# Four weight pairs of a head by seven block products in place of two, in a hybrid recurrent and attention layer

## The chip, the cores and the metric

The kernel runs on one core of a Trainium2 chip. The metric is the time of one execution on the device, in microseconds, as the median of three runs. The core's engines are TensorE (PE in the profile; its weight loads are PEld), VectorE (DVE), ScalarE (ACT), GpSimd (POOL) and SyncE (SP). They work side by side and wait for each other by semaphores. SP and POOL issue DMAs.

## What is computed

One decoder layer over 512 tokens and 16 meta tokens in front of them, with 1024 channels and 8 heads of 128 in each of two branches. Cut to what matters:

```
u = rmsnorm(h, norm_g)
proj = einsum('bld,de->ble', u, w_in)                 # 1024 -> 10 x 1024
hq, hf, hi, hz, aq, ak, av, az, ga, gb = split(proj)
oA = hgrn2_chunked(hq, log f(hf), 1 - f, hi)           # per head, recurrent
yA = (rmsnorm(oA) * silu(hz)) @ w_branch_a
oB = diff_attention(rope(aq), rope(ak), av, lam)       # per head, two softmaxes
yB = (rmsnorm(oB) * silu(az)) @ w_branch_b
m = sigmoid(ga) * yA + sigmoid(gb) * yB
out = rmsnorm(h + m @ w_out, final_g)                  # the 512 tokens
```

The large part is `proj`. Every projection works on full fp32 values that are split in two: a high part (`w_hi`, `uT_hi`, rounded to the type that TensorE multiplies in one pass) and the rest (`w_lo`, `uT_lo`). One product of a 128x128 weight tile is three matmuls: high by high, low by high and high by low (`three`).

## The kernel before, in words

A head needs eight blocks of 128 weight columns: HF, HQ (the recurrent forget gate and query), AK, AQ (attention key and query), HI, HZ (recurrent value and output gate), AV, AZ (attention value and output gate). The kernel makes them in two ways.

A **unit** is one block of 128 columns against all eight tiles of the contraction, over all 528 or 512 tokens: 48 matmuls of 256 to 272 columns or 24 of 512. In every head HI, HZ, AV and AZ are units (`unit`, `section`), in this order.

A **pair** is two blocks (HF with HQ, AK with AQ) computed at once by the seven products of a 2x2 block multiplication (Strassen's scheme in Winograd's form). The two block dimensions are the two halves of the tokens and the two halves of the contraction. Each **part** j = 0 to 6 is one product: four weight tiles by 256 or 272 columns, so 12 matmuls (`part`). Parts 0 and 3 add into one bank of PSUM and are block 11 of the result (`c_11`); the others end in two more banks and are combined with VectorE's `comb_75`, `comb_16`, `comb_21`, `comb_22`, `comb_12`, after ScalarE has saved two products to SBUF (`save_p1`, `save_p5`). Parts 1, 2, 5 and 6 need sums of weight blocks, in place in the loaded weights: two by accumulating DMAs from POOL (`add_s1`, `add_s3`), two by VectorE (`sum_2`, `sum_4`). The token sides of parts 1, 2, 4 and 5 are `t_hi`, `t_lo`, made once.

ScalarE makes every high weight part (`unit_hi`, `part_hi`). The low part is VectorE's subtraction (`part_lo`), or ScalarE writes the negated high part and POOL adds the weights by an accumulating DMA (`add_unit`, `add_part`). Before, five of seven parts of a pair are lowered by VectorE, and three of four units by DMA (the fourth, HI, in two halves by VectorE).

The order of work is fixed by hand. TensorE's instruction stream of a head is 60 slots (`head`, `SLOTS_A_HEAD`): 32 of units, 28 of half parts. Behind the slots that the tables `HG_AT` and `AT_AT` name, the stream holds the small matmuls of the two mixers: the seven levels of the recurrence (`level`, l1 to l64, each needing VectorE's step of the level before it: `next_level`, then `take_level`), the scores, transposes and outputs. The other engines' streams are written out by hand in the same way, and each engine works strictly along its own stream. A head computes its own HI, HZ, AV, AZ and the HF, HQ, AK, AQ of the next head. Behind eight heads come six pairs of the columns GA, GB (the gates), then the two branch projections and the output projection. All loads of weights come from SP.

## Time and profile before

| | |
|---|---|
| median of 3 runs (lowest to highest) | 728.02 us (727.49 to 728.16) |
| span of the profiled execution | 726.1 us |
| PE busy | 706.2 us (97%) |
| DVE, ACT, POOL busy | 73%, 50%, 16% |
| granted TensorE clock, mean of the core | 0.999 |

The profiled execution is known by its span, from its first to its last instruction, which is 1.9 us under the median of the runs; what lies around the span is taken to stay. Busy time is the union of an engine's instructions. A matmul's own duration contains its way through the array and overlaps the next one, so what a matmul costs in a stream is the distance between starts.

### The profile page before, as it was taken

To read this page: it belongs to the slowest core of one execution; us is meant where nothing else is said; L and a number is where in the kernel's file an instruction comes from. 1 tells how busy PE (TensorE), PEld (TensorE's weight loads), DVE (VectorE), ACT (ScalarE), POOL (GpSimd) and SP (SyncE) were. 2 spreads that over 40 slices of the span, in tenths; PEclk is the share of its full clock that TensorE was granted. 3 is DMA by queue.
4 is the path that set the end of the run, shared out by engine and by line. 5 is a ranking of instruction groups with operands and counts; after the bars stand their busy time and mean duration, and the time that the engine had idled before them with its cause. 6 is when DMAs were issued, how large, how long until landed. Compare 5 with 4: busy or idle time off the path is not lost.

```text
span 726.1 us, 14492 instructions
## 1 busy us (share of the span) xinstructions
PE 706.2 (97%) x4953; PEld 651.9 (90%) x4953; DVE 531.6 (73%) x1241; ACT 364.5 (50%) x739; POOL 113.8 (16%) x134
## 2 busy tenths in 40 slices
PE   3999999999999999999999999999999999999996
PEld 3998999999899899999989989999999988888885
DVE  5799888788768768878876876887688872744442
ACT  5454663663564565366356456537566662222232
POOL 2011220221121122122112112212211000000000
PEclk9999999999999999999999999999999999999999
DMA  7355556557556555655745755555777653236103
GB/s 274 116 132 131 131 131 159 131 116 181 108 130 173 130 130 130 159 130 122 182 101 131 184 119 130 139 159 128 155 197 207 195 173 116 88 105 214 59 0 116
DMA packets 37251, 101.86 MB, mean 140 GB/s; under 512 B 4162, under 2 KB 4564, under 8 KB 37220
## 3 DMA queue, kind: packets, MB, share of 16 engines
q1 hardware_dynamic: 22068, 67.77, 27.0%
q0 software_dynamic: 14400, 32.51, 25.7%
q10 hardware_dynamic: 752, 1.18, 0.5%
q8 instruction: 18, 0.29, 0.2%
q14 instruction: 13, 0.11, 0.0%
HBM read 66.84 MB, written 2.10 MB: 95 GB/s over the span
## 4 chain that ended last, share of the span: by engine, by line
PE 90%; DMA 3%; DVE 3%; issue 2%; ACT 1%; POOL 0%; SPq 0%; POOLq 0%; DVEq 0%; ACTq 0%
PE ps L673 25%; PE ps L674 24%; PE ps L675 24%; PE ps L848 3%; PE ps L918 3%; PE ps L944 2%; PE ps L834 1%; PE ps L935 1%; DMA w_raw<-in_w_in 1%; PE ps L882 1%; PE ps L881 1%; PE ps L864 1%; PE ps L945 1%; PE ps L889 1%; DMA x_in<-in_x 1%
## 5 line engine op out<-in xcount | busy, mean ns | idle before, releaser
L673 PE MATMUL ps<-uT_hi,w_hi 128*128 128x272 f32 (+3 forms) x704 | 226.4, 322 | 0.0
L674 PE MATMUL ps<-uT_lo,w_hi 128*128 128x272 f32 (+3 forms) x704 | 215.6, 306 | 0.0
L675 PE MATMUL ps<-uT_hi,w_lo 128*128 128x272 f32 (+3 forms) x704 | 215.5, 306 | 0.0
L673 PEld LDWEIGHTS ps<-uT_hi,w_hi 128*128 128x128 f32 x704 | 133.4, 190 | 7.6 <-issue 1.2
L675 PEld LDWEIGHTS ps<-uT_hi,w_lo 128*128 128x128 f32 x704 | 133.1, 189 | 5.9
L674 PEld LDWEIGHTS ps<-uT_lo,w_hi 128*128 128x128 f32 x704 | 133.4, 189 | 4.6
L673 PE MATMUL ps<-t_hi,w_hi 128*128 128x256 f32 x352 | 103.1, 293 | 1.5 <-DVE p L1578 0.8
L675 PE MATMUL ps<-t_hi,w_lo 128*128 128x256 f32 x352 | 99.5, 283 | 0.0
L674 PE MATMUL ps<-t_lo,w_hi 128*128 128x256 f32 x352 | 99.4, 282 | 0.0
L325 ACT ACTIVATE w_hi<-w_raw 128x1024 fp32r<-128x1024 f32 x53 | 56.0, 1059 | 79.1 <-PE ps L675 55.1
L364 ACT ACTIVATE w_hi<-w_raw 128x512 fp32r<-128x512 f32 x132 | 78.0, 623 | 17.7 <-DMA w_raw<-w_raw 7.8
L332 DVE TENSOR_TENSOR w_lo<-w_raw,w_hi 128x1024 fp32r<-128x1024 f32 x29 | 35.5, 1223 | 54.6 <-ACT w_hi L325 54.5
L371 DVE TENSOR_TENSOR w_lo<-w_raw,w_hi 128x512 fp32r<-128x512 f32 x100 | 67.0, 685 | 10.1 <-ACT w_hi L364 9.9
L673 PEld LDWEIGHTS ps<-t_hi,w_hi 128*128 128x128 f32 x352 | 67.0, 190 | 4.3 <-issue 3.1
L1189 ACT ACTIVATE e<-e,small 128x144 f32<-128x144 f32 (+3 forms) x64 | 36.2, 566 | 61.8 <-DVE small L1794 61.8
L674 PEld LDWEIGHTS ps<-t_lo,w_hi 128*128 128x128 f32 x352 | 67.0, 190 | 0.0
L675 PEld LDWEIGHTS ps<-t_hi,w_lo 128*128 128x128 f32 x352 | 66.9, 190 | 0.0
L619 POOL DMA_DIRECT2D w_lo<-w_raw x32 | 31.6, 987 | 97.4 <-ACT w_lo L366 95.1
L593 POOL DMA_DIRECT2D w_lo<-w_raw x24 | 21.4, 893 | 124.8 <-ACT w_lo L327 124.8
L624 POOL TENSOR_TENSOR small<-small 128x4 f32<-128x4 f32 x16 | 19.6, 1228 | 115.4 <-DVE small L1736 60.3
L613 POOL DMA_DIRECT2D w_sum<-w_raw x22 | 19.3, 876 | 97.4 <-DMA w_raw<-in_w_in 97.2
L848 PE MATMUL ps<-qq,sq 128*128 128x128 f32 x192 | 29.3, 275 | 0.5 <-DVE sq L1697 0.5
(243 smaller groups left out, 1437.4 us busy)
## 6 DMA issues: line engine op xcount, KB each, us to landing
w_raw<-in_w_in SPq DMA_DIRECT2D x71, 512.0 KB, 3.6
w_lo<-w_raw POOLq DMA_DIRECT2D x24, 512.0 KB, 4.6
w_lo<-w_raw POOLq DMA_DIRECT2D x32, 256.0 KB, 3.9
w_sum<-in_w_in SPq DMA_DIRECT2D x29, 256.0 KB, 2.9
w_sum<-w_raw POOLq DMA_DIRECT2D x22, 256.0 KB, 3.4
w_raw<-w_raw POOLq DMA_DIRECT2D x22, 256.0 KB, 4.4
w_raw<-in_w_branch_a SPq DMA_DIRECT2D x8, 512.0 KB, 3.4
w_raw<-in_w_branch_b SPq DMA_DIRECT2D x8, 512.0 KB, 3.2
```

Source lines behind the costliest of these rows:

```text
L325: act.activation(w_hi[:, slot, :], raw_at(r), ACT.Copy).then_inc(hi_ready, 1)
L332: eng.tensor_tensor(w_lo[:, slot, :], raw_at(r), w_hi[:, slot, :].bitcast(F32), ALU.subtract).then_inc(ready, 1)
L364: act.activation(blk(w_hi, i), part_src(r, j), ACT.Copy).then_inc(pair_hi, 1)
L371: dve.tensor_tensor(blk(w_lo, i), part_src(r, j), blk(w_hi, i).bitcast(F32), ALU.subtract).then_inc(pair_lo, 1)
L593: pool.dma_start(w_lo[:, slot, :], raw_at(r), accum_op=ALU.add).then_inc(unit_added[n], 16)
L619: pool.dma_start(blk(w_lo, i), part_src(r, j), accum_op=ALU.add).then_inc(part_added[j - 3], 16)
L673: pe.matmul(dst, w[0], rhs[0], start=start, stop=False, skip_group_check=True)
L674: pe.matmul(dst, w[0], rhs[1], start=False, stop=False, skip_group_check=True)
L675: return pe.matmul(dst, w[1], rhs[0], start=False, stop=stop, skip_group_check=True)
L848: mm = pe.matmul(walk(dst, i * P // 2, (P, 2), (m, P // (2 * m)), (1, m)), k_mix[:, i, :], walk(qq[:, i * P:], m, (HALF - m, 2), (2 * m, P ...
L918: mm = pe.matmul(bank(B_S + comp)[:, at_s:at_s + n - at_k], q[half[comp], q_b], k[half[comp], at_k:n], start=i == 0 and b != 1, stop=i == ...
L1189: act.activation(e, e, ACT.Exp, bias=nb[:, at_nb:at_nb + 1], scale=-1.0, accum_out=(l_1, l_2)[comp][:, b:b + 1]).then_inc(exp_done, 1)
```

## The change

All four pairs of a head are computed by seven products. HI with HZ and AV with AZ become pairs like the two others, so a head is 56 slots of half parts, in the order 0, 1, (4 of the pair before), 5, 3, 6, 2. Head 0 keeps its units HI, HZ, AV, AZ. Only pairs of even and odd number differ, in the set of buffers (two sets of loaded weights, `SETS`) and in the bank (1 or 3) that is their chain. In that bank parts 5, 2 and 4 add up, on top of minus part 0, which ScalarE writes there first (`seed`). What the banks hold between the parts is read out on the way: `save_p50` after part 5, `c22` after part 2, `c_21` after part 4, `c12` from bank 2. Parts 2, 3 and 4 of every pair are lowered by DMA, parts 0, 1, 5, 6 by VectorE; of the gates' pairs all but the first have all parts by VectorE, as before. The scaling of the outputs by their norm and the affine maps to `f` and `kk` go from VectorE to ScalarE. The seven levels alternate between banks 6 and 7.

The diff, cut to its core:

```diff
-SLOTS = 8
-RAW = 2
+SLOTS = 7
+SETS = 2
-COLS = (HI, HZ, AV, AZ)
-PAIRS = ((HF, HQ), (AK, AQ))
+PAIRS = ((HI, HZ), (AV, AZ), (HF, HQ), (AK, AQ))
+PART_ORDER = (0, 1, 4, 5, 3, 6, 2)
-BY_VECTOR = (0, 1, 2, 5, 6)
+BY_VECTOR = (0, 1, 5, 6)
+BY_DMA = (3, 2, 4)
-SLOTS_A_HEAD = 8 * UNITS + 4 * PARTS
+SLOTS_FIRST = 8 * UNITS + 4 * PARTS - 2
+SLOTS_A_HEAD = 2 * PARTS * PAIRS_A_HEAD
-HG_AT = dict(zip(HG_STEPS, (2, 7, 11, 14, 17, 20, 23, 26, 30, 33, 36, 42)))
-AT_AT = dict(zip(AT_STEPS, (21, 21, 30, 33, 33, 36, 37, 40, 42, 44, 46, 51, 53, 59)))
+HG_AT = dict(zip(HG_STEPS, (2, 7, 11, 14, 18, 22, 25, 28, 30, 33, 35, 52)))
+AT_AT = dict(zip(AT_STEPS, (26, 26, 28, 33, 33, 35, 35, 37, 37, 39, 42, 46, 48, 55)))
...
+            act.wait_ge(w_used, used(pr, j) - PARTS)
+            act.activation(part_at(w_hi, j), part_src(pr, j), ACT.Copy).then_inc(pair_hi[j], 1)
+            if j in BY_DMA and not pr.gate:
+                act.activation(part_at(w_lo, j), part_src(pr, j), ACT.Copy, scale=-1.0).then_inc(part_neg[j], 1)
...
+            def load_pair(pr, before, h, cols):
+
+                sp.wait_ge(pair_lo[6], before.q + 1)
+                sp.sem_inc(slot_free, 1)
+                base_21(pr, h, cols)
+                columns(h, cols[0], 2 * pr.set)
+                sp.wait_ge(*low_done(before, 2))
+                sp.sem_inc(slot_free, 1)
+                half_columns(h, cols[1], 2 * pr.set + 1, 0).then_inc(w_loaded[2 * pr.set + 1], 16)
+                sp.wait_ge(*low_done(before, 4))
+                sp.sem_inc(slot_free, 1)
+                half_columns(h, cols[1], 2 * pr.set + 1, 1).then_inc(late_loaded[pr.set], 16)
...
+                    elif j == 5:
+                        pe.wait_ge(seeded, pr.q + 1)
+                    elif j == 2:
+                        pe.wait_ge(p50_saved, pr.q + 1)
+                    elif j == 6:
+                        pe.wait_ge(p1_saved, pr.q + 1)
+                    elif j == 4:
+                        pe.wait_ge(c22_out, pr.q + 1)
...
+                        dst = bank(2)[:, 0:HALF] if j == 1 else chain_of(pr)
...
+                    last = three(dst, w, rhs, j in (0, 1) and k == 0, k == KT // 2 - 1)
...
+            def seed(pr, normed=None):
+
+                act.wait_ge(w_used, used(pr, 0))
...
+                act.activation(chain_of(pr), bank(0)[:, META:META + HALF], ACT.Copy, scale=-1.0) \
+                    .then_inc(seeded, 1)
...
+            def c22(pr, dst):
+
+                dve.wait_ge(w_used, used(pr, 2))
+                dve.wait_ge(p1_saved, pr.q + 1)
+                both(dst, chain_of(pr), p_1, c22_out)
...
+                def steady():
+
+                    c_22(3, True)
+                    sum_4(dve, p_0)
+                    turn_pairs(kT[:, :], 0)
+                    next_level(1)
+                    part_lo(dve, p_0, 6)
+                    add_pairs(kT[:, :]).then_inc(rotated, 1)
+                    next_level(2, 0)
+                    part_lo(dve, p_1_, 0, 1)
+                    take_level(1)
+                    sum_2(dve, p_1_)
+                    dve.wait_ge(lvl_taken, 7 * h + 1)
+                    rotated_lo(0)
+                    take_level(2)
+                    q_given()
+                    next_level(4)
+                    swap_pairs(qT[:, :])
+                    c_12(0)
+                    c_22(0)
+                    take_level(3)
+                    part_lo(dve, p_1_, 5)
+                    next_level(8)
```

On VectorE, in the loop over the heads, from behind the step of level 2 to the step of level 4 (`kk` and `qq` are the level's operands, `w_lo` low weights, `w_raw` a weight sum, `kT_lo` the low part of the rotated key), before:

```order
L1703 TENSOR_TENSOR tt<-tt 128x128
L1720 COPY_PREDICATED aa<-masks,ps 128x2x64x2
L1772 REGISTER_ALU
L1773 TENSOR_TENSOR kT_lo<-kT,kT_hi 128x528 [waits rothi_ready]
L1757 STREAM_SHUFFLE e_95<-qT 128x512
L1618 REGISTER_ALU
L1683 REGISTER_ALU [waits dve_own]
L1684 REGISTER_ALU [waits lvl_taken]
L1694 TENSOR_TENSOR kk<-kk,tt 128x2x32x4 [waits hg_done]
```

and in the changed kernel at the same place:

```order
L386 TENSOR_TENSOR w_lo<-w_raw,w_hi 128x512 [waits pair_hi0]
L386 TENSOR_TENSOR w_lo<-w_sum,w_hi 128x512 [waits pair_hi1]
L1871 COPY_PREDICATED aa<-masks,ps 128x2x128
L391 ISA
L395 TENSOR_TENSOR w_raw<-w_sum,w_raw 128x512 [waits pair_lo0,s3_added1,s1_added1]
L1916 REGISTER_ALU [waits lvl_taken]
L1917 TENSOR_TENSOR kT_lo<-kT,kT_hi 128x528 [waits rothi_ready]
L1871 COPY_PREDICATED aa<-masks,ps 128x2x64x2
L1770 REGISTER_ALU [waits c22_out,c21_taken]
L1832 REGISTER_ALU [waits dve_own]
L1835 REGISTER_ALU [waits lvl_taken,lvl_ready]
L1845 TENSOR_TENSOR kk<-kk,tt 128x2x32x4 [waits hg_done]
```

Two low weight parts, a weight sum and the taking of level 1 now stand between the two steps; the shuffle of `qT` moved behind them.

On POOL, in its loop over the heads, the second half of the head's list before (`part_neg` is ScalarE's negated high part, L619 the addition of a low part, L613 and L603 those of a weight sum):

```order
L613 DMA w_sum<-w_raw 128x512 [waits w_loaded1]
L603 DMA w_raw<-w_raw 128x512 [waits w_loaded0,w_loaded1]
L617 ISA
L619 DMA w_lo<-w_raw 128x512 [waits part_neg]
L617 REGISTER_ALU
L619 DMA w_lo<-w_raw 128x512 [waits part_neg]
L624 TENSOR_TENSOR small<-small 128x4 [waits ms_ready]
L649 REGISTER_ALU
L649 COMPARE_AND_BRANCH
```

and the end of the same loop in the changed kernel (L605 adds a low part, L590 and L598 weight sums):

```order
L605 DMA w_lo<-w_raw 128x512 [waits part_neg4]
L609 REGISTER_ALU
L610 TENSOR_TENSOR small<-small 128x4 [waits ms_ready]
L603 ISA
L605 DMA w_lo<-w_raw 128x512 [waits part_neg3]
L590 DMA w_raw<-w_raw 128x512 [waits w_loaded2,w_loaded3]
L605 DMA w_lo<-w_raw 128x512 [waits part_neg2]
L598 DMA w_sum<-w_raw 128x512 [waits base_loaded1,late_loaded1]
L650 REGISTER_ALU
L650 COMPARE_AND_BRANCH
```

The additions for the first pair of the next head (`part_neg3` and `part_neg2` behind L610) are now the last thing of a head on POOL, and the small power `small<-small` stands in front of them. A head has 20 additions instead of 11.

## Rows read from the trace of the kernel before

**Rows 1.** the page, busy time and share of each engine

```profile
PE 706.2 (97%) x4953; PEld 651.9 (90%) x4953; DVE 531.6 (73%) x1241; ACT 364.5 (50%) x739; POOL 113.8 (16%) x134
```

**Rows 2.** stretches of the span: busy time of each engine, granted clock, DMA share, GB/s

```profile
46.00:107.00 61.00, 60.55 (x459) 56.75 (x459) 53.43 (x133) 34.22 (x74) 12.13 (x13) 1.00 0.55 133
107.00:528.00 421.00, 420.68 (x3201) 395.92 (x3199) 330.13 (x879) 225.81 (x497) 85.18 (x92) 1.00 0.58 140
510.00:546.00 36.00, 34.45 (x284) 33.35 (x283) 28.18 (x59) 22.30 (x49) 7.13 (x8) 1.00 0.70 176
287.80:348.10 60.30, 60.30 (x461) 56.82 (x460) 47.80 (x128) 32.61 (x72) 12.08 (x13) 1.00 0.60 142
```

**Rows 3.** the waits of PE: for whom, us in total, times, longest

```profile
PE ps L673 <- DVE p L1578: 0.8, 1, 0.8
PE ps L848 <- DVE sq L1697: 0.5, 1, 0.5
```

**Rows 4.** timeline of PE in head 4: start us, us, instruction

```profile
290.42 0.28 PE L673 MATMUL ps<-uT_hi,w_hi 128*128 128x272 f32 x1
...
291.15 0.29 PE L673 MATMUL ps<-uT_hi,w_hi 128*128 128x272 f32 x1
...
293.98 0.40 PE L674 MATMUL ps<-uT_lo,w_hi 128*128 128x512 f32 x1
...
295.62 0.40 PE L675 MATMUL ps<-uT_hi,w_lo 128*128 128x512 f32 x1
...
314.83 0.28 PE L674 MATMUL ps<-uT_lo,w_hi 128*128 128x272 f32 x1
...
316.09 0.29 PE L675 MATMUL ps<-uT_hi,w_lo 128*128 128x272 f32 x1
...
318.61 0.28 PE L675 MATMUL ps<-t_hi,w_lo 128*128 128x256 f32 x1
...
320.41 0.28 PE L675 MATMUL ps<-t_hi,w_lo 128*128 128x256 f32 x1
```

**Rows 5.** timeline of DVE in the same head

```profile
289.16 0.43 DVE L1694 TENSOR_TENSOR kk<-kk,f 128x256 f32<-128x256 f32 x1 [1.33 <-PE ps L834]
...
291.14 0.73 DVE L1720 COPY_PREDICATED aa<-masks,ps 128x256 f32<-128x256 uint8 x1
...
293.67 0.42 DVE L1694 TENSOR_TENSOR kk<-kk,tt 128x256 f32<-128x256 f32 x1
...
294.75 0.73 DVE L1720 COPY_PREDICATED aa<-masks,ps 128x256 f32<-128x256 uint8 x1
...
313.19 0.68 DVE L371 TENSOR_TENSOR w_lo<-w_raw,w_hi 128x512 fp32r<-128x512 f32 x1
313.79 0.68 DVE L371 TENSOR_TENSOR w_lo<-w_sum,w_hi 128x512 fp32r<-128x512 f32 x1
```

**Rows 6.** timeline of ACT in the same head

```profile
302.29 1.14 ACT L364 ACTIVATE w_hi<-w_raw 128x512 fp32r<-128x512 f32 x2
303.33 0.62 ACT L366 ACTIVATE w_lo<-w_raw 128x512 fp32r<-128x512 f32 x1
...
324.00 0.38 ACT L1197 ACTIVATE pT<-ps 128x256 f32<-128x256 f32 x1 [0.89 <-PE ps L938]
324.28 0.25 ACT L1198 ACTIVATE pT<-ps 16x128 f32<-16x128 f32 x1
```

**Rows 7.** timeline of POOL in the same head

```profile
317.19 0.86 POOL L619 DMA_DIRECT2D w_lo<-w_raw  x1 [7.28 <-ACT w_lo L366]
```

**Rows 8.** the page, DMA queues: packets, MB, share of 16 engines

```profile
q1 hardware_dynamic: 22068, 67.77, 27.0%
q0 software_dynamic: 14400, 32.51, 25.7%
```

**Rows 9.** the page, DMA issues: KB each, median us from issue to landing

```profile
w_lo<-w_raw POOLq DMA_DIRECT2D x32, 256.0 KB, 3.9
```

**Rows 10.** the four L619 additions of head 1, issue to landing

```profile
DMA to landing us min/median/max: 3.3/3.8/5.7
```

More of the change, by code:

```diff
@@ L489, in _, with loads_of_head @@
+            def loads_of_head(h, last):
+                for p in range(PAIRS_A_HEAD):
+                    before = pair_of(h, p - 2) if p >= 2 else pair_of(h - 1, p + 2)
+                    if last and p >= 2:
+                        load_pair(pair_of(h, p), before, p - 2, (GA, GB))
+                    else:
+                        load_pair(pair_of(h, p), before, h + 1 if p >= 2 else h, PAIRS[p])
             for i in range(CH):
@@ new lines, in _ @@
+            add_unit(0, 1, 1)
+            add_unit(1, 2, 2)
+            add_unit(2, 3, 3)
+            p_2, p_3 = pair_of(0, 2), pair_of(0, 3)
+            add_s3(p_2)
+            add_s1(p_2)
+            add_part(p_2, 3)
+            add_s3(p_3)
+            add_part(p_2, 2)
+            add_s1(p_3)
+            second_half_of(0)
+            with pool.Fori(0, HEADS - 1) as i:
+                head(i + 1)
+            add_part(gate_pair(0), 4)
+            for n in range(2, GATES):
+                add_s3(gate_pair(n))
+                add_s1(gate_pair(n))
@@ L946, in attend, with values_ready, mixers @@
                     .then_inc(at_done, 1)
+            def values_ready(h, branch):
+                if isinstance(h, int) and h == 0:
+                    pe.wait_ge(sec_taken, UNITS + 1 + branch)
+                else:
+                    pe.wait_ge(c11_taken, pair_of(h, branch).q + 1)
+                    pe.wait_ge(c12_out, pair_of(h, branch).q + 1)
+            def mixers(h, t, hg_at, at_at):
+                for e in range(1, 8):
+                    if t == hg_at[HG_STEPS[e - 1]]:
+                        level(h, e)
+                for b in range(2):
+                    if t == at_at[f"s{b}"]:
+                        scores(h, b)
+                if t == hg_at["keys"]:
+                    keys_token_major(h)
+                if t == at_at["values"]:
+                    values_ready(h, 1)
+                    pe.wait_ge(lvl_taken, 7 * h + 7)
+                    values_token_major(vT_b, B_T, at_done)
+                if t == hg_at["values"]:
+                    values_ready(h, 0)
+                    pe.wait_ge(ktok_ready, h + 1)
+                    values_token_major(vT_a, B_A, hg_done)
+                if t == hg_at["sums"]:
+                    state_sums(h)
+                if t == hg_at["out"]:
+                    outputs(h)
+                if t == hg_at["turn"]:
+                    turn(h, 0, B_S, hg_done)
+                for b in range(CH):
+                    if t == at_at[f"t{b}"]:
+                        turn_probs(h, b)
+                    if b >= 2 and t == at_at[f"s{b}"]:
+                        scores(h, b)
+                    if t == at_at[f"a{b}"]:
+                        attend(h, b)
+                if t == at_at["turn"]:
+                    turn(h, 1, B_T, at_done)
@@ L983, in head @@
-                    if t == AT_AT["turn"]:
-                        turn(h, 1, B_T, at_done)
-            with pe.Fori(0, HEADS - 1) as h:
-                head(h, False)
+                    p, step = t // (2 * PARTS), t % (2 * PARTS)
+                    j = PART_ORDER[step // 2]
+                    if j != 4:
+                        pr = pair_of(h, p)
+                    else:
+                        pr = pair_of(h, p - 1) if p > 0 else pair_of(h - 1, PAIRS_A_HEAD - 1)
+                    part(pr, j, step % 2, not last or p < 2)
```

1368 lines of the change are left out of this document (725 added, 643 removed).

## The prediction

> **What bounds the kernel now.** I read first the busy times: TensorE works 97% of the span, VectorE 73%, ScalarE 50% [rows 1]. The stretches tell where the missing 3% lie: in heads 1 to 7 TensorE idles 0.3 us of 421, in head 0 0.5 us of 61, between the last head and the first gates 1.6 us of 36, and the granted clock is 1.00 in all of them, its upper level of 2.4 GHz [rows 2]. The waits of TensorE inside the work are single ones below 1 us [rows 3]. So TensorE's stream is the bound from the start of head 0 to the end, a head takes 60.1 to 60.3 us (421 / 7 [rows 2] and the stretch of head 4), I use 60.2,, and every matmul less is time, as long as nothing makes TensorE wait.
>
> **What TensorE saves.** The price of a matmul is the distance of starts, not its duration. Six matmuls of 272 and 256 columns in turn take 291.15 - 290.42 = 0.73 us; seven steps of 512 columns take 1.64 us, 0.234 each; ten steps of 272 take 1.26 us, 0.126; fifteen of 256 take 1.80 us, 0.120 [rows 4]. A matmul of 264 columns lies between the last two, I take 0.121. Before, a head's units cost 8 x 0.73 = 5.84 (HI), 24 x 0.234 = 5.62 (HZ), 48 x 0.121 = 5.81 (AV) and 5.62 (AZ), together 22.9 us. As two pairs they are 2 x (24 x 0.126 + 60 x 0.120) = 20.4 us. That is 2.4 us a head, in heads 1 to 7 (head 0 keeps its units), so between 16.3 and 17.2 us with the rounding of the distances; I take **-16.5 us**. The mixers' matmuls are the same. They stand in 19 places of a head instead of 20, which is worth about 0.1 us each; I count nothing. The two slots that head 0 loses are made in head 1, also nothing.
>
> The Trainium skill (page "TensorE: Matmul & The Clock Gate", section "Back-to-back issue gap") puts a warm matmul of N columns at N / 2.4 + 2.5 ns; for 256 columns that is 109 ns where the row has 120. By that rule a head would save about 2.5 us and the change about 17.5 us. The row is taken; it says the same with 1 us less.
>
> **What the other engines get.** VectorE: one step of 512 columns costs 313.79 - 313.19 = 0.60 us, one of 256 about 0.34 [rows 5]. A head gets 4 low parts and 4 sums more (+4.8), 2 combinations less (-0.7), no scaling by the norm (-1.2) and no `f` and `kk` (-1.0): +1.9 us, 49.7 of 57.8 us, 86%. ScalarE: a step of 512 costs (303.33 - 302.29) / 2 = 0.52, one of 256 0.28 [rows 6]. A head has 40 copies of 512 instead of 20 and none of the six of 1024 (taken as 1.04 each: +10.4 - 6.2), 20 of 256 or 272 instead of 6 (+3.9), 8 short ones and two of 528 for the moved work (+2.4), three takes less (-1.1): about +9.5, 42 of 57.8, 73%. POOL issues 20 additions instead of 11 at 0.86 each [rows 7], from 12 to 20 us. DMA: the software queue's share is 0.257 x 726 / 32.51 = 5.7 us of all engines per MB, the hardware queue's 2.9 [rows 8]. A head moves 5.2 MB instead of 3.7 by the first and 5.2 instead of 4.7 by the second, so the share goes from 0.60 [rows 2] to (30 + 15) / 57.8 = 0.78. No engine becomes the bound by its sum. What is at stake is the order in which they meet.
>
> **What can wait.** The new waits of TensorE are the chain's: `seeded` before part 5, `p50_saved` before 2, `p1_saved` before 6, `c22_out` before 4, `c11_taken` and `c12_out` before the next pair's 0 and 1. Each of these has two parts or more between the event and the need, 2 x 2.06 us with the mixers' share (57.8 / 28). One step of ScalarE is 0.3 to 0.5 us, so these hold unless its stream is stuck at something else. The tight place is VectorE at the start of a head. Time 0 is the end of the last head's turn; VectorE reads that at 0.25, then `gated` and `c_22` until 1.3. `sum_4` of the first pair needs part 3 of it added by DMA. Its negated part can start when TensorE has left the slot (part 3 of the pair before ends 3.9 us before time 0) and is written at about -2.4; POOL's issue 0.86 [rows 7], about 0.3 between them, and 3.9 to land [rows 9] make 2.7. So VectorE waits 1.4 us there. From 2.7 on it has `sum_4` 0.6, the rotation's two products 1.3, the step of level 1 2.0 (291.14 - 289.16), a low part 0.6, the rotation's sum 0.6, the step of level 2 1.1 (294.75 - 293.67) [rows 5], two low parts 1.2, the taking of level 1 0.5, a sum 0.6, the key's low part 0.65, the taking of level 2 0.4 and the step of level 4 up to its copy 1.0: 10.6, so 13.3. TensorE wants that for l8 behind slot 14, at 15 x 0.726 + 1.3 (l1) + 2 x 0.46 (l2, l4) = 13.1, then two more levels at the same pace: the step of level 8 is ready at about 16.9 against 16.8. That is 0.2 to 0.4 us with the semaphores, and 0.1 or 0.2 at l16. At l32, l64 and the scores I find VectorE even with TensorE, and from slot 28 on one to five microseconds ahead. In the trace before the same steps have room: VectorE stands idle 1.33 us for l1 [rows 5]. I take **0.55 us a head, +3.9 us** for seven heads. Bounds: nothing, if part 3 lands early or the reading of starts is pessimistic (one step of 0.1 us in each of six), and 2.0 us a head, 14 us, if part 3 needs the 5.7 us of the slowest of four [rows 10] (in POOL's order the first of a head's L619 stands right behind L613 and L603): 1.8 us later, all of it on this chain.
>
> Head 0 has new tables and two sets of buffers that load earlier; its VectorE stream gets two products of the rotation ahead of level 1 and loses one step of 1.2 us there. Priced at 0, with -0.5 to +2. Gates: VectorE has 7 low parts and 2 sums as before, and 2 combinations instead of 5 (-1.0 us of a pair's 10.1), ScalarE 8 short steps more in six pairs; TensorE is full there but for the 1.6 us [rows 2] in which the first gate pairs wait for loads. With two sets and no third, I let that stand: -1.5 to +2, priced at 0. Tail: the same work.
>
> **Sum.** The profiled execution of 726.1 us would become 726.1 - 16.5 + 3.9 = 713.5; with 1.9 us between span and median, **715.5 us**.
>
> **The rivals.**
> 1. *The additions by DMA are late* (12 low parts of a head by DMA instead of 4, share 0.60 to 0.78). The place is `sum_4` of each head's first pair, which is the head of VectorE's chain. Each microsecond over the 3.9 [rows 9] is a microsecond of TensorE at l8, times seven. It is slower than before from the point where the stall of a head passes 2.35 us, so from a landing of 5.7 us on, the slowest of rows 10, as the rule and not the exception; at 6.5 us it is 0.55 + 2.6 a head, 22 us, and the time 728.0 - 16.5 + 22 = 733. For it: POOL issues the addition with a load and another addition right behind. Against it: three additions stand together in POOL's order now too, and the median is 3.9 [rows 9].
> 2. *VectorE and ScalarE pace the heads without a DMA's part.* At 86% and 73% in fixed streams that wait for each other in turn (high part, low part, sum, high part), a wait at one place is paid at the next. If they lose 1.2 to 2 us a head, it is 720 to 725.
> 3. *All is hidden.* No stall at all: 711.5; with the 1.6 us in front of the gates gone too, 710.
>
> By the Trainium skill (page "SBUF — State Buffer", section "Who interferes with whom"), a VectorE instruction with two SBUF inputs keeps GpSimd from reading SBUF, and its copies in the two-port mode lock GpSimd out, so that descriptors of a software DMA come late. Here that would speak for rival 1, since VectorE gets 8 two-input steps and POOL 9 issues more in a head. The trace before does not show it as a cost: the issues of 0.86 stand beside a VectorE that is busy 79% of the head. It moves no chance by itself.
>
> **How the numbers follow.** Forecast 0.66, rival 2 0.15, rival 3 0.09, rival 1 0.10, of which 0.06 is slower than before, 0.01 the same and 0.03 still faster; 0.02 of rival 2 ends at no change. The range that leaves out 2 in 10 is **711.5 to 722**. A measurement of this kernel tells about 0.2%, 1.5 us, from no change: faster (below 726.5) 0.91, same 0.03, slower 0.06.
>
> **What would show it.** Right: a period of 57.8 to 58.8 us between two l1 in heads 1 to 7 (60.2 before); TensorE's idle time at l8 and l16, ended by VectorE's copy `sq<-kk`; VectorE waiting about 1.4 us for `w_lo<-w_raw` at the head's first `sum_4`; DMA share near 0.78. Wrong: waits of TensorE for ScalarE's seed or saves, or for a low weight part or its DMA at parts 2, 3 or 4 (then the weights' chain is late, not the mixers'); landings of L605 above 5 us; a distance of 256-column matmuls other than 0.120 us, which would take the ground from the saving itself.

## The result, and the profile after

The changed kernel takes 734.66 us (median of 4, 733.18 to 735.95), the kernel before 728.09 beside it: a ratio of 1.0093, 95% interval 1.0076 to 1.0111. It is slower by 0.9%. The forecast was 715.5, with 711.5 to 722.

The page after, against [rows 1, 8, 9], with the busy times, the two queues and the landing of the low additions:

```profile
PE 696.1 (95%) x5121; PEld 653.8 (89%) x5121; DVE 534.9 (73%) x1224; ACT 452.7 (62%) x1013; POOL 174.1 (24%) x202
...
q0 software_dynamic: 24192, 44.84, 36.2%
q1 hardware_dynamic: 27972, 71.44, 28.6%
...
w_lo<-w_raw POOLq DMA_DIRECT2D x93, 256.0 KB, 4.4
```

TensorE is busy 10 us less than before in a span that is 7.7 us longer. The waits of PE from the start of head 0 on (for whom, us in total, times, longest), against [rows 3]:

```profile
PE ps L928 <- DVE qT_lo L1917: 6.8, 1, 6.8
PE ps L671 <- ACT p L1202: 6.4, 2, 6.1
PE ps L853 <- DVE sq L1848: 4.3, 7, 1.0
PE ps L671 <- DVE tg L1763: 2.0, 5, 0.6
```

Only the third row, the levels of the heads, was in the sum. The first is one wait, the second almost all one (6.1 of 6.4), at two places that were priced at nothing. Stretches of the span (busy time of each engine, granted clock, DMA share, GB/s): the steady heads, the ten us around the first wait and the ten behind it, the fifteen around the second:

```profile
120.00:484.00 364.00, 359.43 (x2978) 348.66 (x2977) 310.14 (x803) 271.59 (x652) 123.29 (x136) 1.00 0.80 180
56.00:66.00 10.00, 3.23 (x23) 2.80 (x24) 3.30 (x9) 1.63 (x3) 0.87 (x1) 0.79 0.80 205
66.00:76.00 10.00, 10.00 (x70) 9.38 (x69) 8.25 (x32) 3.57 (x11) 0.00 (x0) 0.87 0.01 2
530.00:545.00 15.00, 8.92 (x52) 8.75 (x51) 7.22 (x11) 7.53 (x16) 2.61 (x3) 0.66 0.43 92
```

The heads look as forecast, DMA share 0.80 (0.78 forecast). At the two places TensorE stands still, and then the granted clock is below 1.00: each wait is paid twice.

**Where the time went.** VectorE's product of the identity in level 1 stands once in each head, and the first merge once, behind the gates. Two rows (count, min/median/max ns, first and last start) give the ends of the ledger; the starts between them are from VectorE's timeline.

```profile
L1851 DVE TENSOR_TENSOR aa<-ps,ident x8: 677/682/685, 48.3 to 469.2; 128x512 f32<-128x512 f32 x8
...
L2195 DVE SCALAR_TENSOR_TENSOR t_m<-kk,ps x1: 680/680/680, 625.8 to 625.8; 128x512 f32<-128x512 f32 x1
```

| us | before | forecast | after |
|---|---|---|---|
| l1 of head 0 to l1 of head 1 | 60.99 | 61.0 | 68.59 |
| a head, mean of heads 1 to 6 | 60.26 | 58.5 | 58.72 |
| l1 of head 7 to the first merge | 147.64 | 145.8 | 156.59 |
| merge to the end | 107.7 | 107.7 | 108.0 |

The profiled execution is 20.3 us over the forecast of 713.5: 7.6 in head 0, 10.8 behind head 7's l1, 1.6 in six heads (0.26 each), 0.3 at the end.

**Head 0.** The timeline of four engines (start us, us, instruction, idle before it and what ended it); L598 is POOL's addition s1, L378 ScalarE's high part, L1279 its copy of the rotated q, L928 the scores:

```profile
57.64 0.87 POOL L598 DMA_DIRECT2D w_sum<-w_raw  x1 [1.74 <-issue]
...
51.70 0.63 ACT L378 ACTIVATE w_hi<-w_raw 128x512 fp32r<-128x512 f32 x1
63.15 0.63 ACT L378 ACTIVATE w_hi<-w_sum 128x512 fp32r<-128x512 f32 x1 [10.81 <-DMA w_sum<-w_raw]
63.68 0.61 ACT L1279 ACTIVATE qT_hi<-qT 128x512 fp32r<-128x512 f32 x1
...
55.98 0.69 DVE L1912 TENSOR_TENSOR qT<-qT,e 128x512 f32<-128x512 f32 x1
...
64.33 0.69 DVE L1917 TENSOR_TENSOR qT_lo<-qT,qT_hi 128x512 fp32r<-128x512 f32 x1 [6.70 <-ACT qT_hi L1279]
...
65.07 0.85 PE L928 MATMUL ps<-kT,qT 64*128 64x144 f32 x4 [6.77 <-DVE qT_lo L1917]
```

Read from the bottom: TensorE waits for q's low part, this for its high part, and the high part waits for nothing of its own (q was rotated 56.7 us into the span, L1912): it stands in ScalarE's stream behind `part_hi(p_2, 1)`, which waits for s1. That part is wanted 18 slots later. The loss does not need a late addition: in run 7 below, which has the same head 0, s1 was there 4.1 us after its issue, close to the median of these additions (4.2), and TensorE still waited 4.4 us for q; in runs 2 and 4, at 6.4 and 6.8 us, it waited 8.2 and 8.7.

**The first gates.** The same picture with the save of `p_50` (L1202) in the place of q:

```profile
527.60 0.86 POOL L598 DMA_DIRECT2D w_sum<-w_raw  x1 [2.98 <-issue]
...
534.62 0.63 ACT L378 ACTIVATE w_hi<-w_sum 128x512 fp32r<-128x512 f32 x1 [8.31 <-DMA w_sum<-w_raw]
...
536.47 0.37 ACT L1202 ACTIVATE p<-ps 128x256 f32<-128x256 f32 x1
...
530.62 0.28 PE L673 MATMUL ps<-uT_hi,w_lo 128*128 128x256 f32 x1
536.98 0.55 PE L671 MATMUL ps<-t_hi,w_hi 128*128 128x256 f32 x1 [6.08 <-ACT p L1202]
...
542.66 0.41 PE L673 MATMUL ps<-t_hi,w_lo 128*128 128x256 f32 x1
542.88 0.39 PE L671 MATMUL ps<-t_hi,w_hi 128*128 128x256 f32 x1
```

From 536.98 to 542.88 a matmul of 256 columns comes every 0.213 us, behind it every 0.120: the lower clock level, 1.2 GHz. 28 matmuls at 0.093 us too much are 2.6 us on top of the 6.1. The Trainium skill (page "TensorE: Matmul & The Clock Gate", section "Back-to-back issue gap") has N / 1.2 GHz between starts at the lower level, 213 ns here; the trace agrees.

### The profile page after: what moved, and what is told of

Same layout as the page of the kernel before. It is cut to its first block, busy times and chain, and to the rows that moved or that the text cites. A ratio compares the mean times of both kernels' runs of the same rounds, so it can differ in the third digit from the quotient of the medians.

```text
span 733.8 us, 15603 instructions
## 1 busy us (share of the span) xinstructions
PE 696.1 (95%) x5121; PEld 653.8 (89%) x5121; DVE 534.9 (73%) x1224; ACT 452.7 (62%) x1013; POOL 174.1 (24%) x202
## 4 chain that ended last, share of the span: by engine, by line
PE 71%; DMA 10%; DVE 8%; issue 6%; ACT 3%; SPq 1%; POOL 0%; DVEq 0%; POOLq 0%; ACTq 0%
PE ps L671 19%; PE ps L672 18%; PE ps L673 18%; DMA w_lo<-w_raw 4%; DMA w_raw<-in_w_in 3%; PE ps L853 2%; PE ps L928 2%; DMA w_sum<-w_raw 2%; PE ps L956 2%; DVE aa L1871 1%; DVE w_lo L386 1%; PE ps L945 1%; PE ps L869 1%; DMA x_in<-in_x 1%; PE ps L889 1%
## 5 line engine op out<-in xcount | busy, mean ns | idle before, releaser
L671 PE MATMUL ps<-t_hi,w_hi 128*128 128x256 f32 x576 | 170.8, 297 | 8.4 <-ACT p L1202 6.4
L378 ACT ACTIVATE w_hi<-w_raw 128x512 fp32r<-128x512 f32 x216 | 132.7, 624 | 61.0 <-PE ps L673 34.7
L671 PE MATMUL ps<-uT_hi,w_hi 128*128 128x272 f32 (+3 forms) x536 | 163.5, 305 | 0.0
L673 PE MATMUL ps<-t_hi,w_lo 128*128 128x256 f32 x576 | 163.3, 284 | 0.0
L672 PE MATMUL ps<-t_lo,w_hi 128*128 128x256 f32 x576 | 163.3, 283 | 0.0
L672 PE MATMUL ps<-uT_lo,w_hi 128*128 128x272 f32 (+3 forms) x536 | 156.2, 291 | 0.0
L673 PE MATMUL ps<-uT_hi,w_lo 128*128 128x272 f32 (+3 forms) x536 | 156.1, 291 | 0.0
L605 POOL DMA_DIRECT2D w_lo<-w_raw x93 | 88.3, 949 | 214.8 <-ACT w_lo L380 204.4
L672 PEld LDWEIGHTS ps<-t_lo,w_hi 128*128 128x128 f32 x576 | 110.6, 192 | 0.0
L673 PEld LDWEIGHTS ps<-t_hi,w_lo 128*128 128x128 f32 x576 | 110.4, 192 | 0.0
L380 ACT ACTIVATE w_lo<-w_raw 128x512 fp32r<-128x512 f32 x93 | 57.5, 618 | 0.0
L590 POOL DMA_DIRECT2D w_raw<-w_raw x36 | 34.0, 945 | 79.3 <-DMA w_raw<-in_w_in 77.4
L378 ACT ACTIVATE w_hi<-w_sum 128x512 fp32r<-128x512 f32 x36 | 22.5, 624 | 32.4 <-DMA w_sum<-w_raw 32.2
L598 POOL DMA_DIRECT2D w_sum<-w_raw x36 | 34.0, 946 | 32.6 <-issue 26.8
```

What stands on the lines that cost most here:

```text
L378: act.activation(part_at(w_hi, j), part_src(pr, j), ACT.Copy).then_inc(pair_hi[j], 1)
L380: act.activation(part_at(w_lo, j), part_src(pr, j), ACT.Copy, scale=-1.0).then_inc(part_neg[j], 1)
L590: pool.dma_start(raw_at(r + 1)[:, 0:BLK], raw_at(r)[:, 0:BLK], accum_op=ALU.add) \
L598: pool.dma_start(w_sum[:, pr.set, :], raw_at(2 * pr.set + 1)[:, BLK:], accum_op=ALU.add) \
L605: pool.dma_start(part_at(w_lo, j), part_src(pr, j), accum_op=ALU.add).then_inc(part_added[j], 16)
L671: pe.matmul(dst, w[0], rhs[0], start=start, stop=False, skip_group_check=True)
```

## The experiments

All are edits of the changed kernel; the ledger of each profiled execution follows below the runs.

**1. Head 0's q first.**

```diff
-                part_hi(act, p_2, 0, 1)
+                part_hi(act, p_2, 0)
                 rotated_hi(0, 1)
                 take_first(5)
+                part_hi(act, p_2, 1)
```

> One swap in ScalarE's head 0: the rotated q's high part and the tanh of z stand ahead of part_hi(p_2, 1), which waits for the addition s1 by DMA. Nothing else moves; the transfers are issued as before. Theory (order): TensorE's 6.8 us in front of head 0's scores are the queue behind that wait, since q itself was rotated 56.6 us into the span. The wait falls to 0 to 0.5 us, the stretch at half the granted clock behind it (about 1.8 us of loss) goes as well, s1 still lands near 63 us and nobody waits for it: 726.4, which is 8.3 us less than the changed kernel (725.5 to 728). Rival (DMA): the load of 8.6 us and the additions of 4.8 to 5.5 us make TensorE wait at one of the next places too (part 0 or 1 of p_2, the levels): 731 to 735.

726.07 to 736.49 us in 11 executions, median 728.52 (2 us over the 726.4 expected), ratio 1.0035 (1.0006 to 1.0063); the profiled one took 726.69. In it head 0 takes 60.45 us instead of 68.59, and TensorE waits nowhere from head 0 to head 1. So the order is shown as the cause of head 0's 8.1 us (6.8 of waiting, the rest the clock); the four profiles with the old order have 67.5 to 71.7 us there, all those with the new order 60.1 to 61.4 but for two, which run 11 explains. But the executions spread over 10 us, where 23 of the kernel before in the same comparison lie within 3.5 (726.6 to 730.1); that stayed open until runs 13 and 14.

**2. The first gate pair's order, 3. both.** ScalarE's stream of gate pair 0 (VectorE's: `c12` ahead of `sum_2`):

```diff
                 save_p1(pr)
-                if more:
+                if n > 0 and more:
                     part_hi(act, more, 1)
                 part_hi(act, pr, 4)
                 gate_21(n + 1, before)
                 save_p50(pr)
...
                 gate_11(n + 2, pr)
+                if n == 0:
+                    part_hi(act, more, 1, 5)
```

> Order at the first gate pair alone: ScalarE does part_hi(pr, 4), the gate's tanh, save_p50 and gate_11 ahead of part_hi(more, 1), which waits for s1 by DMA, and VectorE does c12 ahead of sum_2(more). Theory (order): the 6.1 us in front of part 2 go, and what is left is the wait of gate pair 1's part 1 for s1 itself, which lands at 534.6: about 2 to 2.5 us. The half clock behind the 6 us (2.7 us of loss) goes or shrinks, and the second half load of gate pair 2, which waits for part 4's low part, leaves some 8 us earlier, so that the waits of 0.53 and 0.40 us at 553 and 555 go: 727 (726 to 730), against 734.7. Rival (DMA): the transfers themselves are late (s1 took 7.0 us to land), and TensorE waits for part 1 about as long as it waited for part 2: 731 to 735.

733.91 us, ratio 1.0079 (1.0049 to 1.0109): no measurable gain, where 7 us were expected, and the stretch behind head 7's l1 only fell from 156.6 to 154.2. That is little clear of noise: four profiles with the gates' orders unchanged (the changed kernel, runs 1, 4 and 7) have 155.3 to 158.2 there.

> Both orders together (head 0's q, first gate pair). If the two losses are separate places, the gains add: 734.7 - 8.3 - 7.5 = 718.9 (717.5 to 721), faster than the kernel before by 1.2%. If the losses have one cause behind them in the load on the DMA engines, the sum is smaller than the two gains: above 722.

725.72 us, ratio 1.000 (0.997 to 1.003), 12 executions, seven from 723.7 to 726.1 and five from 730.7 to 732.5. My theory of the gates fell by half. The wait for `save_p50` is gone, as said, but TensorE waits for s1 itself, and s1 is later than ever. In the run with both orders:

```profile
518.90 0.33 SPq L486 DMA_DIRECT2D w_sum<-in_w_in  x1
519.28 0.45 SPq L452 DMA_DIRECT2D w_raw<-in_w_in  x1
...
519.05 0.86 POOL L598 DMA_DIRECT2D w_sum<-w_raw  x1 [1.97 <-issue]
...
528.26 0.63 ACT L378 ACTIVATE w_hi<-w_sum 128x512 fp32r<-128x512 f32 x1 [5.88 <-DMA w_sum<-w_raw]
...
529.66 0.58 PE L671 MATMUL ps<-t_hi,w_hi 128*128 128x256 f32 x1 [3.43 <-DVE w_lo L386]
```

9.2 us from issue to use, where the median of these additions is 4.1, beside the loads that SP begins to issue 0.15 us ahead of it.

**4. VectorE's order in the heads.** `swap_pairs(qT)` behind `next_level(8)`, `turn_pairs(qT)` behind `next_level(16)`.

> Changed kernel, heads 1 to 7: VectorE's swap of q's halves stands behind the step of level 8 instead of ahead of it, q's two products behind the step of level 16, its sum ahead of level 32. VectorE's total is the same. Theory (VectorE's chain): TensorE's 4.3 us in seven waits at l8 are VectorE being 0.6 us late there; that step gets 0.7 us of room and the wait goes: 4 us less than the changed kernel, 730.7 (730 to 732). Rival (the sum decides: the delay only moves): TensorE waits at l16, l32 or the scores instead, 733.5 to 735.5.

733.8 us, ratio 1.008 (1.0058 to 1.0101); the waits at the levels 5.3 us instead of 4.3. This tested less than I wrote: the copy that releases l8 is the one of the step of level 4, and everything that I moved stands behind that step. The wait stays at l8 (0.52 us in each head), so nothing behind the step of level 4 has a part in it.

**5. The loads wait for the addition.** Run 3, and on SP ahead of gate pair 2's loads `sp.wait_ge(s1_added[1], sets_done(gate_pair(1)))`.

> Both orders of the run before (head 0's q, first gate pair), and the loads of gate pair 2 wait until s1 of gate pair 1 has landed. In the run with both orders s1 was issued at 519.05 and landed 9.2 us later, beside a MB of loads issued from 518.9 on; TensorE waited 3.4 us for part 1, 1.35 us at the next part 4, and ran 12 matmuls at 0.213 us. Theory (the loads crowd the addition): s1 lands in 4 to 5 us, all three go, 6 us less than both orders alone: 719 to 720. Rival (the addition is slow by itself, or something else is in its way): s1 still takes 8 to 9 us and the time stays at 724 to 726, or rises, because gate pair 2 comes later.

723.37 us (721.94 to 725.46), ratio 0.9938 (0.9918 to 0.9957), where run 3 had 1.000. s1 lands in 3.6 us instead of 9.2:

```profile
519.85 0.86 POOL L600 DMA_DIRECT2D w_sum<-w_raw  x1 [1.08 <-issue]
...
523.55 0.33 SPq L486 DMA_DIRECT2D w_sum<-in_w_in  x1
...
531.12 0.36 PE L673 MATMUL ps<-t_hi,w_hi 128*128 128x256 f32 x1 [1.77 <-DVE tg L1768]
```

The wait of 3.43 is gone, one of 1.77 for `c22` stands one step on. The stretch behind head 7's l1 fell by 2.9 us, half of the 6 expected. The short wait is paid twice as well. Within 1 us TensorE is at the lower level (busy times, granted clock 0.50):

```profile
532.00:535.00 3.00, 3.00 (x16) 3.00 (x15) 0.17 (x1) 0.00 (x0) 0.00 (x0) 0.50 1.04 182
```

That loads crowd an addition is shown; that it was the whole of the gates' loss is not.

**6. c22 ahead of the splits.** Run 5, and VectorE's `split_lo(0, n)` (1.2 us) moved out from ahead of `c22`, the first branch's low part behind the last `c22`. In a steady gate pair of run 3, TensorE:

```profile
554.52 0.28 PE L673 MATMUL ps<-t_hi,w_lo 128*128 128x256 f32 x1
555.01 0.36 PE L671 MATMUL ps<-t_hi,w_hi 128*128 128x256 f32 x1 [0.21 <-DVE tg L1766]
555.21 0.28 PE L672 MATMUL ps<-t_lo,w_hi 128*128 128x256 f32 x1
```

A wait of 0.21 us costs 0.49 + 0.20 - 2 x 0.12 = 0.45.

> As the run with the waiting loads, and in VectorE's gates the splits of oa (1.2 us each) stand behind the next pair's part 1 instead of ahead of c22, and the first branch unit's low part behind the last c22. Theory: the period of 10.45 us of a steady gate pair (10.02 before the change) is TensorE at part 4 waiting 0.21 us for c22, with a gap of 0.49 us in place of 0.12 and a slow first matmul; the period falls to 10.1 and the 0.64 us in front of the last part 4 goes: 2.0 to 2.5 us less than the run with the waiting loads. Rival (a cycle over ScalarE and VectorE paces the pair): the period stays at 10.4.

724.18 us, ratio 0.9964 (0.9942 to 0.9986), not better than run 5. The steady waits are gone (10.02 us from seed to seed, 10.46 in the changed kernel), but gate pair 1 now waits 4.4 us for `save_p50`, behind its own `part_hi(more, 1)`: run 2's place, one pair later. The s1 waited for there left 0.15 us behind the next pair's first load and took 7.8 us; in run 5 it left 1.0 us ahead and took 5.4, and this wait was not there.

**7. k's low part behind the step of level 4**, on top of run 4; **8. all edits so far.**

```diff
-                    part_lo(dve, p_1_, 0, 1)
+                    part_lo(dve, p_1_, 0)
                     take_level(1)
-                    sum_2(dve, p_1_)
+                    part_lo(dve, p_1_, 1)
                     dve.wait_ge(lvl_taken, 7 * h + 1)
-                    rotated_lo(0)
+                    sum_2(dve, p_1_)
                     take_level(2)
                     q_given()
                     next_level(4)
+                    rotated_lo(0)
```

> The changed kernel with q's rotation later (as in the run that moved only that, which moved nothing ahead of the step that releases l8), and now also the key's low part (0.62 us) behind the step of level 4. That step's copy releases l8. Theory (VectorE's chain): TensorE's 0.5 to 0.6 us at l8 of heads 1 to 7 go and no other level waits: the period falls from 58.7 to 58.0 us, 4 to 5 us less than the changed kernel: 730. Rival (the heads are paced by the transfers, through sum_4's wait): VectorE only waits longer for the DMA and the period stays.

734.86 us, ratio 1.0089 (1.0067 to 1.0111). The waits at the levels fell from 4.3 us to 1.0, as said, but the period only from 58.72 to 58.47, not to 58.0. The total did not fall by the 4 to 5 us expected; the profiled execution has 158.2 us behind head 7's l1, where nothing was changed, and that is more than the heads gained.

> All of it: head 0's q, the first gate pair's order, the waiting loads, c22 ahead of the splits, and the heads' order with q and the key's low part later. If the losses are separate and the theories hold, the gains add: 719.5 - 2.3 - 4.5 = 712.7 (711.5 to 715), which is the saving that was forecast for TensorE with almost nothing given back. If the transfers' lateness only comes out elsewhere: above 717.

721.97 us, ratio 0.9947 (0.9917 to 0.9977); eight of 12 executions from 720.6 to 722.7, three from 730.4 to 732.7. The heads take 58.35 us without a wait of TensorE that the profile shows, so 58.3 is what its stream takes, not 57.8. Pair 1 waits 4.25 us for `save_p50`.

**9. The second gate pair too**, its order and its loads' wait.

> The run with all edits, and the order of the first gate pair now at the second too (part_hi(pr, 4), save_p50 and gate_11 ahead of the next pair's part_hi 1; c12 ahead of sum_2), with the loads of gate pair 3 waiting for s1 of pair 2 as well. In the run with all edits TensorE waited 4.25 us for save_p50 at the second pair, queued behind part_hi(more, 1), whose s1 took 7.6 us beside the loads of pair 3, and the clock fell to half again. Theory (same cause one pair later): both go, s1 of pair 2 lands in 4 to 5.5 us, 5.5 us less than all edits: 716 to 717. It should also end the slow third of the executions (730 to 733), if these are the ones in which such a wait came a second time. Rival (the late transfer is only paid one step later, at part 1 or at pair 3): 720 to 722.

727.11 us, ratio 0.9995 (0.9967 to 1.0022), where 716 to 717 was expected, and six of 12 executions above 728: no better than run 8, if not worse, and my theory was wrong here. The loads of gate pair 3, held back to 534.8, made pair 3 late in turn, and the wait of 4.2 us went on to pair 2. A turn of a buffer set (load, s1, high and low part) is as long as a gate pair; time taken from one step was taken from the next.

**10. Fewer additions.** Run 9 with part 4's low parts all by VectorE (`BY_VECTOR = (0, 1, 5, 6, 4)`).

> As the run with the second gate, but the low part of part 4 is made by VectorE everywhere, instead of by ScalarE's negated copy and an addition by DMA in heads: 4 steps of 0.6 us a head more on VectorE (50.0 to 52.4 of some 58), 4 negated copies of 0.52 less on ScalarE, 4 of 12 low additions of 256 KB less on the software queue. Theory (VectorE is the tight engine, the additions are well placed): TensorE waits for VectorE at one or two places more, 58.3 becomes 58.8 to 59.3 us a head, 3 to 7 us slower than the run with the second gate. Rival (the transfers are what delays the heads): the additions left land sooner, VectorE waits less for them, and it is even or up to 2 us faster.

732.37 us, ratio 1.006 (1.004 to 1.008), 59.87 us a head. The waits of PE in the heads:

```profile
PE ps L669 <- DVE w_lo L386: 11.5, 7, 1.7
```

The additions by DMA earn their place in the heads: VectorE has no room for 2.4 us more.

**11. Part 4 by VectorE for two pairs only, 12. without the wait of the loads.** The second half loads of gate pairs 1 and 2 wait for these parts. Run 11 keeps the second gate pair's order of run 9, but not the wait of pair 3's loads.

> All edits as before the second gate's waiting load (that wait of gate pair 3's loads is taken out again; the order of the second gate pair stays), and the low part of part 4 is made by VectorE for two pairs only, the last pair of head 7 and gate pair 0: the second half load of gate pairs 1 and 2 waits for exactly these two parts, and so far for an addition by DMA of 4 to 6 us. Theory (the two buffer sets are turned around through these additions): the half loads leave 3 to 5 us sooner, s1 of gate pairs 1 and 2 is issued sooner, the waits of 4.2 us for save_p50 with their half clock go, and from head 7's l1 to the first merge it is 148 to 150 us (152.2 with all edits, 147.7 before the change): 715 to 717. Rival (the load itself and s1 take the time, 4.4 and 4 to 8 us, so that two sets are too few whatever frees them): 152 us and more, 719.5 to 723.

> The same without the wait of gate pair 2's loads for s1 of gate pair 1. Theory (loads crowd the addition): that s1 takes 7 to 9 us again instead of 4, but since it starts sooner TensorE loses only 1 to 3 us more at gate pair 1's part 1: 717 to 719. Rival: s1 is out before the loads start, and the two kernels take the same time within 1 us.

Run 11: 717.81 us, ratio 0.9874 (0.9847 to 0.9900), eight of 12 executions from 716.0 to 719.6, four from 724.5 to 727.1; the stretch behind head 7's l1 is 149.2 us. Run 12: 723.16 us, ratio 0.9896 (0.9859 to 0.9932), three executions from 715.8 to 718.2 and four from 723.2 to 725.5, the stretch 146.6. The additions of two low parts held the sets: without them the stretch is 3.0 us shorter than in run 8, which differs in the second pair's order too, and run 10 is 3.5 us shorter than run 9, with the same orders. And with s1 gone 2.0 us before the loads (521.79 against 523.80), holding the loads back only costs, 2.5 us here and 3.0 between runs 13 and 15. The profiled execution of run 11 is of the longer group. It shows what these are, in head 0:

```profile
58.03 0.87 POOL L606 DMA_DIRECT2D w_sum<-w_raw  x1 [2.03 <-issue]
...
66.23 0.63 ACT L384 ACTIVATE w_hi<-w_sum 128x512 fp32r<-128x512 f32 x1 [8.42 <-DMA w_sum<-w_raw]
66.77 0.40 ACT L1269 ACTIVATE e<-e,small 128x144 f32<-128x144 f32 x1
...
67.69 0.16 DVE L1960 RECIPROCAL small<-small 128x1 f32<-128x1 f32 x1 [5.81 <-ACT e L1269]
```

The stretch around it (busy times, granted clock 0.66):

```profile
66.00:76.00 10.00, 5.93 (x22) 4.92 (x23) 7.46 (x21) 3.97 (x12) 1.76 (x2) 0.66 0.31 54
```

s1 of p_2 is used 8.2 us after its issue (4.2 in run 1). Behind it in ScalarE's stream now stand the exps, behind these VectorE's probabilities, behind them the step of level 32. TensorE waits 5.1 us and runs on at half the clock: 67.8 us for head 0.

**13. The queue taken away, 14. the crowd taken away.** Run 13 is run 11 with

```diff
                 take_first(5)
-                part_hi(act, p_2, 1)
                 exps(0, 0)
                 exps(0, 1)
                 take_first(6)
+                part_hi(act, p_2, 1)
```

and VectorE's low part 1 behind `next_level(64)`. Run 14 is run 11 with the loads of p_3 waiting for s1 of p_2.

> As the run with part 4 by VectorE late (716.0 to 719.6 us in two thirds of its executions, 724.5 to 727.1 in the others), and in head 0 ScalarE's part_hi(p_2, 1) stands behind the first exps and VectorE's low part 1 behind the step of level 64. The profiled execution of that run is of the longer kind: s1 of p_2 landed 8.2 us after its issue at 58.0, the first exps stood behind it in ScalarE's stream, the probabilities behind these in VectorE's, the step of level 32 behind them, and TensorE waited 5.15 us and then ran at half the clock. Theory (the longer executions are those in which this addition lands later than about 63 us): they are gone, 716 to 719 throughout, median 716.5. Rival (they come from somewhere else, the additions in the heads or the gates): a third of the executions stays at 724 and more.

> As the run with part 4 by VectorE late, with head 0's streams unchanged, but the loads of p_3 (issued at 57.9, 0.1 us ahead of the addition's 58.0) wait until s1 of p_2 has landed. Theory (loads crowd the addition): s1 lands in 4 to 5 us, before 63, in every execution, so the longer kind goes here too without any change of order: 716 to 719. Rival (the addition is late for another reason, as the three additions of units or its own time): a third of the executions stays at 724 and more.

Run 13: 716.73 us (716.09 to 720.17), ratio 0.9858 (0.9837 to 0.9879). Run 14: 718.47 us (716.27 to 720.03), ratio 0.9872 (0.9851 to 0.9893). Neither has a longer execution in five, which would happen by chance about one time in eight each if a third of the executions were still long (an estimate, 2/3 to the fifth power). In run 13 the addition is late all the same, and costs nothing; in run 14 it lands in 3.5 us:

```profile
59.17 0.87 POOL L606 DMA_DIRECT2D w_sum<-w_raw  x1 [2.35 <-issue]
...
67.28 0.63 ACT L384 ACTIVATE w_hi<-w_sum 128x512 fp32r<-128x512 f32 x1 [0.95 <-DMA w_sum<-w_raw]
```

```profile
57.43 0.87 POOL L607 DMA_DIRECT2D w_sum<-w_raw  x1 [1.58 <-issue]
...
60.93 0.63 ACT L384 ACTIVATE w_hi<-w_sum 128x512 fp32r<-128x512 f32 x1 [2.96 <-DMA w_sum<-w_raw]
```

**15. Run 13 without the wait of gate pair 2's loads.**

> As the run with the exps first, without the wait of gate pair 2's loads. In the pair of runs that differ by this wait alone, the stretch from head 7's l1 to the first merge was 146.7 us without it and 149.2 with it, since s1 of gate pair 1 had left 2 us before these loads. Theory (both findings hold together): no execution of the longer kind, and 2 to 3 us less than the run with the exps first: 714 to 715, in the span 60.4 for head 0, 58.3 to 58.5 a head and 147 for the last stretch. Rival (the short stretch without the wait was luck in one profiled execution): 716 to 718, as with the wait.

716.2 us (715.98 to 717.2, 5 executions), ratio 0.9847 (0.983 to 0.9863): the fastest, and within 1 us of the forecast, though not the 714 to 715 expected; it can't be told from run 13. Its profiled execution has a span of 714.1. All waits of PE from head 0 on:

```profile
PE ps L678 <- DVE tg L1773: 1.9, 3, 0.6
PE ps L678 <- ACT p L1209: 0.7, 1, 0.7
```

**The ledger of the profiled executions**, us:

| run | span | head 0 | a head, 1 to 6 | l1 of head 7 to merge |
|---|---|---|---|---|
| before | 726.1 | 60.99 | 60.26 | 147.7 |
| after | 733.8 | 68.59 | 58.72 | 156.6 |
| 1, q first | 724.8 | 60.45 | 58.70 | 155.3 |
| 2, first gate | 734.5 | 71.38 | 58.71 | 154.2 |
| 3, both | 723.0 | 61.27 | 58.63 | 153.7 |
| 4, q later | 735.4 | 71.69 | 58.61 | 155.3 |
| 5, loads wait | 722.1 | 61.40 | 58.71 | 150.9 |
| 6, c22 first | 723.2 | 60.44 | 58.76 | 153.3 |
| 7, k later | 732.6 | 67.47 | 58.47 | 158.2 |
| 8, all | 719.6 | 60.50 | 58.35 | 152.3 |
| 9, second gate | 723.8 | 60.42 | 58.57 | 154.8 |
| 10, four by VectorE | 727.4 | 60.11 | 59.87 | 151.3 |
| 11, four late | 723.3 | 67.77 | 58.41 | 149.2 |
| 12, no wait of the loads | 721.7 | 68.10 | 58.47 | 146.6 |
| 13, exps first | 716.7 | 60.42 | 58.32 | 149.7 |
| 14, p_3's loads wait | 716.4 | 60.53 | 58.35 | 149.9 |
| 15, the fastest | 714.1 | 60.53 | 58.43 | 146.7 |

## Why the prediction was wrong

- **TensorE's saving, -2.4 us a head.** Right in kind, too large: 60.26 - 58.3 = 2.0, in heads without a visible wait. The sum of the distances between starts over one head says the same: the units' matmuls take 45.0 us before and 42.9 in run 8 (2.1 less), the mixers' 15.1 and 15.2. The term was built from distances in the middle of a run of equal matmuls; over the head a 256-column matmul costs 0.123 before and 0.126 in run 8, because the first one behind a mixer step takes 0.20. That is 2.8 us over seven heads. (The prediction's own prices give 22.9 - 20.4 = 2.5 a head, of which it took 2.4.)
- **VectorE's chain, +0.55 us a head.** Right: 4.3 us in seven waits, ended by `sq<-kk`, at l8. The wait ahead of it was smaller than said (VectorE lost 0.5 to 1.6 us for the addition, 0.8 on average, not 1.4). But taking 3.3 us of these waits away gave 1.5 in six heads.
- **"Head 0 ... Priced at 0, with -0.5 to +2."** This step failed: +7.6 us. I had counted what each stream of head 0 gets more, and not looked at what stands behind a wait: in the new table `part_hi(p_2, 1)` is one call ahead of q. What is queued behind a waiting instruction was worked out for the start of the steady heads and left out here.
- **"With two sets and no third, I let that stand: -1.5 to +2, priced at 0."** This failed too: with head 7, +10.8 us. In the kernel before, the odd gate pairs had buffers of their own; after, the loads of the first three gate pairs wait for low parts of the pair two before of which two are added by DMA, s1 waits for the load, and `save_p50` stands behind s1 in ScalarE's stream. No single edit gives the 10.8 back. In the order of the runs, the profiles give about 2 for the first pair's order (run 2 against the changed kernel, run 3 against run 1) and 3.0 to 3.5 for two low parts made by VectorE in place of additions; all edits together bring 156.6 to 146.7. How the rest divides stays open, since one profile of an unchanged stretch can differ by 3 us from the next.
- **A wait has a second price that was in no term**, the clock: 1.3 us in head 0 (8.1 less 6.8), 2.6 in the gates; in run 7, whose wait in head 0 is 4.4 us, it is 2.6 there (67.47 less 60.45 less 4.4).
- **"Each of these has two parts or more between the event and the need."** True of the heads. In the gates two parts are 2.9 us, and `c22` behind `split_lo` missed it in each pair.
- **Rival 1, the additions late.** It named the right mechanism at the wrong place. The 733 us that it gave are nearly those measured, but by luck: the low additions land in 4.4 us at the median (7.1 at most from head 1 on), which costs the heads little, and one addition in head 0 and one in the gates did it. Its chance of 0.10 rested on the heads' median, where the question was what waits behind each single addition. Rival 2 (engines pace the heads) did not happen; rival 3 neither. That VectorE's two-input steps hold up POOL's issues of additions does not show here: the issue of a low part takes 0.95 us on average, 0.99 before.

With the orders mended and two low parts moved from DMA to VectorE, the change is 1.5% faster than the kernel before. That this is within 1 us of the forecast is partly luck: in run 15 a head takes 58.43 us, as the forecast's sum had it (58.5), but with a smaller saving (2.0 us, not 2.4) and almost none of the waits at the levels that the forecast priced at 0.55.

What stays open: why run 7's shorter waits gave back only half of their time, and how rare the longer executions are in runs 13 to 15 (none in 15 executions, where about 5 were to be expected; run 11 itself was not repeated beside them, and its two groups were seen on another chip). A third buffer set for the gates wasn't tried.

## What to carry to other kernels

When a transfer becomes a step of a chain, go through each in-order stream for the instruction that waits for it, and list everything behind it, at the transfer's usual landing first and then at its slowest; the first use after a start-up and the last stage, where tables are special, first of all. Put the waiting instruction as late as its own need allows: here one order of head 0 cost 4.4 us of waiting even at a landing of 4.1, and the next cost nothing at 4 us and 7 at 8, and then the kernel has two times. And if two buffers are turned around through several transfers in a row, add up the whole turn against the time of a stage, since a wait moved inside the turn comes out at the next pair.
